# Output products as one 512-column and one 256-column matmul

## The reference

```python
x = x + sqrelu_mlp(rms_norm(x, norm_ffn[i]), ffn_w1[i], ffn_w2[i])      # twice: down_0, down_1
h = h + 0.5 * swiglu_ffn(rmsnorm(h, ffn1_norm[i]), ffn1_w_in[i], ffn1_w_out[i])   # four times: out_0 to out_3
```

## Time and profile before

| what | value |
|---|---|
| median of 3 runs | 1557.24 us |
| profiled execution, its own time | 1556.84 us |
| its span, first to last instruction | 1555.1 us |
| PE busy | 1541.5 us (99%), 12856 matmuls |
| DVE busy | 1041.9 us (67%) |
| ACT busy | 849.8 us (55%) |
| mean DMA rate | 181 GB/s |
| granted TensorE clock | 1.00 |

### The profile page before, as it was taken

How to read it: one execution, slowest core, us unless ns; L and a number is a source line. 1 busy time by engine, 2 the same in 40 slices (tenths; PEclk the granted TensorE clock), 3 DMA queues, 4 the chain that set the end, 5 groups by cost and what they waited for, 6 DMA issues and landing times.

```text
span 1555.1 us, 35183 instructions
## 1 busy us (share of the span) xinstructions
PE 1541.5 (99%) x12856; PEld 1502.0 (97%) x12856; DVE 1041.9 (67%) x1751; ACT 849.8 (55%) x1301; POOL 124.1 (8%) x123
## 2 busy tenths in 40 slices
PE   9999999999999999999999999999999999999999
PEld 8899999988999999999999999989999988999999
DVE  7677765643876557666787766678576656676664
ACT  6776554546665445445445555556555547655543
POOL 1830000036000000000000000000000032200000
PEclk9999999999999999999999999999999999999999
DMA  7246666554566566666666666656566981065564
GB/s 242 71 123 193 197 192 197 169 168 148 183 194 197 188 199 190 195 193 202 193 204 191 200 191 192 211 179 208 188 192 195 229 210 55 15 203 190 192 201 149
DMA packets 80784, 281.02 MB, mean 181 GB/s; under 512 B 8880, under 2 KB 12464, under 8 KB 80688
## 3 DMA queue, kind: packets, MB, share of 16 engines
q1 hardware_dynamic: 76800, 274.78, 56.2%
q10 hardware_dynamic: 3888, 4.85, 1.7%
HBM read 278.03 MB, written 1.57 MB: 180 GB/s over the span
## 4 chain that ended last, share of the span: by engine, by line
PE 93%; DVE 4%; DMA 2%; ACT 1%; issue 1%; SPq 0%; DVEq 0%; ACTq 0%
PE psum L1731 27%; PE psum L1735 27%; PE psum L1732 27%; DMA raw<-tiles 2%; PE psum L1862 2%; PE psum L1864 2%; PE psum L1863 2%; PE psum L2151 1%; PE psum L2102 1%; DVE w_lo L1018 1%; PE psum L2135 1%; PE psum L2049 0%; ACT w_hi L551 0%; PE psum L1926 0%; PE psum L1916 0%
## 5 line engine op out<-in xcount | busy, mean ns | idle before, releaser
L551 ACT ACTIVATE w_hi<-raw 128x1024 fp32r<-128x1024 f32 x518 | 547.1, 1058 | 483.1 <-PE psum L1735 423.6
L1018 DVE TENSOR_TENSOR w_lo<-raw,w_hi 128x1024 fp32r<-128x1024 f32 x484 | 592.2, 1224 | 247.7 <-ACT w_hi L551 247.1
L1731 PE MATMUL psum<-xs,w_hi 128*128 128x256 f32 x1928 | 535.8, 278 | 2.1 <-DVE w_lo L1018 2.1
L1735 PE MATMUL psum<-xs,w_lo 128*128 128x256 f32 x1928 | 533.0, 276 | 0.0
L1732 PE MATMUL psum<-xs,w_hi 128*128 128x256 f32 x1928 | 532.8, 276 | 0.0
L1731 PEld LDWEIGHTS psum<-xs,w_hi 128*128 128x128 f32 x1928 | 361.9, 188 | 3.1 <-DVE w_lo L1018 2.5
L1732 PEld LDWEIGHTS psum<-xs,w_hi 128*128 128x128 f32 x1928 | 361.9, 188 | 0.3
L1735 PEld LDWEIGHTS psum<-xs,w_lo 128*128 128x128 f32 x1928 | 361.8, 188 | 0.0
L1735 PE MATMUL psum<-hs,w_lo 128*128 128x256 f32 x1280 | 353.3, 276 | 0.0
L1731 PE MATMUL psum<-hs,w_hi 128*128 128x256 f32 x1280 | 353.3, 276 | 0.0
L1732 PE MATMUL psum<-hs,w_hi 128*128 128x256 f32 x1280 | 353.3, 276 | 0.0
(11 more groups left out here) (284 smaller groups left out, 1464.9 us busy)
## 6 DMA issues: line engine op xcount, KB each, us to landing
raw<-tiles SPq DMA_DIRECT2D x518, 512.0 KB, 4.3
bias<-bias_dram ACTq DMA_DIRECT2D x8, 256.0 KB, 8.6
x<-x_in SPq DMA_DIRECT2D x4, 256.0 KB, 5.2
w1c_all<-w1c_k ACTq DMA_DIRECT2D x4, 256.0 KB, 4.3
w1c_all<-w1c_v ACTq DMA_DIRECT2D x4, 256.0 KB, 5.8
y_out<-x SPq DMA_DIRECT2D x8, 128.0 KB, 3.5
con<-consts SPq DMA_DIRECT2D x1, 771.0 KB, 8.9
bias_dram<-bias_row ACTq DMA_DIRECT2D x1, 512.0 KB, 7.1
```

The costliest lines, as they stand in the source:

```text
L551: act.activation(w_hi[s][:, :], raw[s][:, :], ACT.Copy).then_inc(hi_ready, 1)
L1018: dve.tensor_tensor(w_lo[s][:, :], raw[s][:, :], hi_of(w_hi[s][:, :]), ALU.subtract).then_inc(lo_ready, 1)
L1731: pe.matmul(out, w_hi[s][:, c:c + P], x_hi, start=first, stop=False)
L1735: return pe.matmul(out, w_lo[s][:, c:c + P], x_hi, start=False, stop=last)
```

## The change

In the six stages of `residual` TensorE uses a new `product`: w_hi is multiplied with x_hi and x_lo side by side in one matmul of 512 columns that fills the whole bank, and w_lo*x_hi is added to the first half. So a bank holds two sums, in its two halves. ACT copies the second half into `half[b]`, and DVE adds it to the first half before it scales the result. `residual_one`, `feature` and all other products stay as they were. `half_ready` is now counted in these stages too, and `r_scaled` is a new semaphore between the scaling and the addition to x.

```diff
-            if kind == "up":
+            if kind == "up" or name in SCALED:
                 n_half += outs
@@ ACT, residual
-                        for j in range(per):
+                        b = (o0 + u) % 4
+                        for j in range(per - 1):
                             split(t0 + u * per + j + RING, i * per)
+                        act.wait_ge(tile_done, i * (4 * per) + (t0 + (u + 1) * per))
+                        act.wait_ge(out_read, i * 4 + (o0 + u - 3))
+                        act.activation(half[b][:, :], bank(b, S, 2 * S), ACT.Copy).then_inc(half_ready, 1)
+                        split(t0 + u * per + per - 1 + RING, i * per)
@@ DVE, residual
-                        dve.wait_ge(tile_done, i * (4 * per) + (t0 + (u + 1) * per))
-                        dve.tensor_tensor(f, bank(b, 0, S), rs[:, :], ALU.mult).then_inc(out_read, 1)
+                        dve.wait_ge(half_ready, i * 4 + (half0[name] + u + 1))
+                        dve.tensor_tensor(f, bank(b, 0, S), half[b][:, :], ALU.add).then_inc(out_read, 1)
                         dve.wait_ge(out_read, i * 4 + (o0 + u + 1))
+                        dve.tensor_tensor(f, f, rs[:, :], ALU.mult).then_inc(r_scaled, 1)
+                        dve.wait_ge(r_scaled, i * 4 + (x0 + u + 1))
                         dve.tensor_tensor(xo, f, xo, ALU.add).then_inc(x_ready, 1)
@@ TensorE
+            def product(out_bank, lhs, k, src, first, last):
+                s, c = lhs
+                both, x_hi = src[:, k * 2 * S:(k + 1) * 2 * S], src[:, k * 2 * S:k * 2 * S + S]
+                pe.matmul(bank(out_bank), w_hi[s][:, c:c + P], both, start=first, stop=False)
+                return pe.matmul(bank(out_bank, 0, S), w_lo[s][:, c:c + P], x_hi, start=False, stop=last)
@@ TensorE, residual
-                            ins = narrow_product((o0 + o) % 4, (t % RING, k * P), c, src, c == 0, c == chunks - 1)
+                            ins = product((o0 + o) % 4, (t % RING, k * P), c, src, c == 0, c == chunks - 1)
```

More of the change, by code:

```diff
@@ L216, in build @@
         sil_ready = sem("sil_ready")
-        x_ready = sem("x_ready")
+        r_scaled, x_ready = sem("r_scaled"), sem("x_ready")
         dve_step = sem("dve_step")
@@ L584, in residual @@
             def residual(name, per, outs=KD, between=None):
-                t0 = TILE0[name]
+                t0, o0 = TILE0[name], OUT0[name]
                 last = name == RES[-1]
```

## The result

The changed kernel takes 1584.59 us (median of 3 runs, 1582.73 to 1584.86) against 1557.24: ratio 1.017, 95% interval [1.0153, 1.0187], 27.3 us slower. I had forecast 10.3 us slower. The span went from 1555.1 to 1582.8 us, by 27.7.

What follows compares the result with a forecast made beforehand. TensorE was taken to bound the kernel. To the profiled 1556.84 us came 8.1 for products, 1.3 for stage-end waits and 0.9 at the end, 1567.1, with 0.4 for the median 1567.5 us; range 1551 to 1578 us.

Steps and rivals of the forecast that it cites:

- What bounds the kernel: Whole kernel: TensorE bounds it, busy 1541.5 of 1555.1 us; three 256-column matmuls take 0.340 or 0.3533 us a product.
- Part 1: TensorE in the six changed stages: a product takes 0.2333 + 0.1133 = 0.3467 us, 0.0067 more, x 1216 = +8.1 us.
- my upper bound of 0.3511: Product in the six changed stages if its 256-column matmul falls into the slow beat: 0.2333 + 0.1178, +13.5 us.
- the untouched stages: `up` and `glu` stages: they keep 0.340 us a product, as line 1724 sets each one's beat anew.
- part 4: Stage ends: TensorE waits 0.45 us behind `down_0`, `down_1` and `out_0`, 1.3 us; at the very end 0.9 us more.
- Rival C: Six changed stages: the slow beat comes back, 0.3511 us a product, +13.5 + 2.2, 1573 us; chance 0.16.
- worse form: `up` and `glu` stages: stalls shift their beat too, 1920 products cost 0.0133 more, +25 us, 1598 us; chance 0.04.
- Rival A: Six changed stages: the weight load was the price, 512 columns take 0.2133 us, -11.7, 1545.5 us; chance 0.20.
- The rule of the Trainium skill: Matmul gap N/2.4 + 2.5 ns for bf16, some 216 ns at 512 columns; product 0.325 us, change worth -18 us.
- Rival B: Six changed stages: no difference at the product, 512 columns cost 0.2267 us; only stage ends, +2.2, 1559.5 us; chance 0.16.
- Parts 2, 3 and 5: Per output, ACT's copy 0.38 us and DVE's operation 0.42 us lie beside TensorE; tile supply costs 0, at most 1 us.

Runs made afterwards that it cites:

- the experiment with the steps alone: Against the changed kernel, TensorE kept the three 256-column matmuls in all stages, with ACT's copy and DVE's addition left in: 1576.50 us, 1.0126 of the kernel before.
- 384+384: Against the kernel before, two matmuls a product of other widths in each of the six stages, 384 and 384 columns in `out_2`: 1579.81 us in all.

## Why the prediction was wrong

*What bounds the kernel* was right: TensorE, by the starts of its matmuls, and the two beats of the three 256-column matmuls decide the result.

*Part 1, the price of a product, is the first step that failed.* I added two rows from different company: 0.2333 from an unbroken run of 512-column matmuls and 0.1133 from the fast beat of 256-column ones. The first held, the second did not: in all six stages, and in `out_3` alone too, which was entered at the fast beat, the 256-column matmul behind one of 512 took 0.120. The product comes to 0.3533, above even my upper bound of 0.3511, and the term was 16.2 us instead of 8.1. Why it is 0.120 is not shown. It isn't simply the slow beat, though the product's price is the same here: the slow beat has 0.1178, and at 128 modulo 512 the product stays at 0.3533 where three narrow matmuls take 0.360. A warning stood in the profile: the earlier trace rows show that 0.1133 is not a price of a matmul but of a state.

*A term that I had put at nothing is the second: the untouched stages.* I wrote that the `up` and `glu` stages keep 0.340. `cin`, `cout` and `glu_1`, 608 products, went to the slow beat, 8.1 us. With the error of part 1 alone the time would have been some 1576 us. My reason, that each of these stages sets its beat anew with line 1724, was wrong. `glu_2` doesn't run that line at all, and where it runs once the beat was handed on, or, behind a wait, came out either way; the earlier trace rows are from a stage where it runs three times. The stage ends of part 4, which I priced by their wait alone at 1.3 us, had 17.5 us hanging on them in the experiment with the steps alone.

*Rival C* (the slow beat comes back) was the nearest, with 1573 us, and a part of its "worse form", to which I gave 0.04, came with it. I had taken those 25 us as all or nothing; the `up` stages, `glu_0`, `glu_2` and `glu_3` stayed fast, and `cin` and `cout` weren't in its count.

*Rival A* (the weight load is the price) fell: with one load fewer a product got slower, and 384+384, with two loads, was above 0.340 too. The rule of the Trainium skill that I had weighed ("TensorE: Matmul & The Clock Gate", "Back-to-back issue gap") gives 0.216 us for 512 columns. That section calls it the gap of an isolated matmul, which I hadn't said; the rows here, streams in which every matmul has its load, had 0.229 to 0.237, and 0.28 in front of 128 columns. *Rival B* fell with it.

*Parts 2, 3 and 5* held: ACT's copy 0.38 us and DVE 0.41 us behind its start, 0.46 and 0.58 us from one DVE step to the next, and no stall for tiles in `out_2` with the products (0.3533 throughout). *Part 4* was near in its own terms: waits of 0.3, 0.3 and 0.45 us where I had 0.45 three times (0.99 less 0.59 is 0.40, so that was a little high by my own figures), some 0.6 us behind them that I hadn't counted, and 0.9 us at the end.

## What to carry to other kernels

Take the price of a matmul from starts, and ask of each such row in which company it was measured: a pace may belong to a sequence, not to an instruction, and a change of the sequence then costs more than the sum of its parts. Before giving up a pace that a kernel has found, look at all stages downstream: a wait of half a microsecond can change their pace, and the wait table shows the wait alone. A state that one trace shows unbroken may have been handed on from stage to stage, and then nothing in that trace says what restores it. And where the pace hangs on the place of a tile in SBUF, compare two forms of a loop at more than one place, since the better form changed here with 320 bytes of padding.

## What the runs showed of the hardware

- With the activations at 448, 192 or 320 modulo 512 bytes, rows of 256-column fp32r matmuls, each with its own load of 128x128, keep one of two paces at the full granted clock: 0.1133 or 0.1178 us a matmul. In these traces they stay in it until another kind of matmul or a wait comes between. The same instructions can have either pace in two executions (`wo_m`, `glu_0`). Three matmuls of 60 columns moved them from the slow to the fast one in `up_0` and in `cin`.
- The place of the moving operand modulo 128 bytes goes with whether the faster one is found (at 64 in three places, not at 0 in three), and without it a product takes 0.356 (at 0 modulo 512) or 0.360 us (at 128 and 384).
- A 512-column matmul takes 0.229 us from its start to the next one in a row of its own kind with `hs` (512+512), 0.2333 in the token-major stages and in front of 256 columns, and 0.28 in front of 128, and 384 columns take 0.173: the pace of a mixed row isn't the sum of the paces of unmixed ones.
- What sets the beats physically is open. No run measured the interplay of loads and streams by itself; that it is such an interplay is only a guess.
